# A decoder block on one core: the program's beginning in another order, with one accumulator for shift's sums

## The chip, the cores and the metric

The kernel runs on 1 core of one Trainium2 chip. The metric is device time in microseconds (us), from one execution of the program to its end; lower is better. The engines are PE (TensorE, the matmuls, with its weight loads shown as PEld), DVE (VectorE), ACT (ScalarE), POOL (GpSimd) and SP (SyncE, which here only issues DMAs). Each engine runs its own list of instructions in order and waits on semaphores for the others.

## The reference

One decoder block on 512 tokens of width 2048, float32. What matters for the beginning of the program:

```python
mod = c @ w_mod + b_mod                                   # w_mod: 2048 x 6144
shift, scale, gate = jnp.split(mod, 3, axis=-1)
u = x * (1.0 + scale[:, None, :]) + shift[:, None, :]
proj = u @ w_in                                           # w_in: 2048 x 12288
q, k, v, z_a, cb, cc, cx, z_b, g_a, g_b = jnp.split(proj, SEG_SPLITS, axis=-1)
...                                                       # attention, convolution, gated merge
out = h @ w_out
r = ALPHA * x + gate[:, None, :] * out                    # then a LayerNorm
```

## The kernel before

**Products.** Float32 products are made of rounded halves: for each weight tile ACT writes a rounded copy (`w_hi`, line 492) and DVE the remainder (`w_lo`, line 762, raw minus rounded), the same is done to the activations (`act_hi`, `act_lo`), and PE makes three matmuls of 512 columns (lines 1239 to 1241) for each product. Weights come in units of 1 MB into two slots of `raw`; a unit is two "halves", a half is 24 matmuls (6 for each of four 128-row tiles n = 0 to 3). `w_hi` and `w_lo` have four slots, so half f can be rounded once half f-4 is done. PE must have `lo_ready` for each half.

**Groups.** To begin before all of `u` is there, the program opens with eight groups g. A group takes 256 columns of `scale`: four chunks of `w_mod` (512 KB each, line 373), one pair of tiles of x (512 KB, `x_in`, line 398) and 896 KB of `w_in` (`raw`, lines 406 and 407). DVE multiplies the 16 row blocks of the chunks by `c` and adds them into two accumulators `mod_sum` in turn (lines 786 and 789, here called the sums); PE adds these over the partitions with one-column float32 matmuls (line 1288, here a reduction); DVE adds the bias (`mod`, line 808, here columns); ACT writes `act_hi` (line 537) and DVE `act_lo` (line 825) of x times (1 + scale); PE then does one half into `acc` and one gate half (18 matmuls) into `sc`. These products lack the shift, whose part is added much later by `bias_acc`.

**Then** come two halves into `misc`, the eight halves of G2 (more gate columns, f = G2 to G2+7), and the eight halves of Q0 (the first attention head, f = Q0 to Q0+7), and then the loop over heads begins (HEAD0). Beside G2 and Q0 the `shift` part of `mod` is made in the same way: 16 chunks of 1 MB (line 385), DVE's sums (512 columns wide), four reductions that PE makes ahead of the halves named in `SHIFT_BEFORE`, DVE's columns (line 816), then ACT's `add_shift` (line 564) and DVE's `shifted_lo` (line 833). Half Q0+s needs tiles 2s and 2s+1 of the shifted activations.

**Ahead of the heads.** After the fourth columns DVE does the lambda dots, the angles, `bring_down(cos)`, `bring_down(sin)` and a memset of `gate` (line 949, 2048 wide). ACT waits for that memset before it issues the DMA of `b_mod` into `gate`; then it rounds HEAD0+1 and HEAD0+2 and empties the four banks of `acc` (`drain_head`, `q_raw` first). PE's first half of HEAD0 waits for bank 0 to be emptied, by the copy to `q_raw`.

**Order.** Nothing is scheduled by a tool: each engine's order is written out by hand. SP's order is also the order of the DMAs in its one queue. `wait_raw(i, per, u)` lets unit u be loaded when the unit two before it has been subtracted; a shift chunk waits for the sums of the chunk that was in its slot.

## Time and profile before

| | us |
|---|---|
| median of 3 runs | 1517.66 (1517.55 to 1519.46) |
| the profiled execution | 1517.38 |
| its span in the profile | 1515.7 |
| PE busy | 1477.4 (97%) |
| DVE busy | 858.5 (57%) |
| ACT busy | 511.1 (34%) |
| PE's granted clock, mean | 0.995 |

A row of the timeline gives start, duration, engine, line, operation, output and inputs, the number of instructions in it, and in brackets the idle time before it with what ended it. Matmul durations overlap, since matmuls are pipelined: the time from start to start is what one costs. A granted clock of 1.00 is 2.4 GHz and 0.50 is 1.2 GHz.

### The profile page before, as it was taken

The page shows a single profiled execution, that of the slowest core. Times are in us where ns is not written, and L with a number is a line of the kernel's source. Part 1 is how long each engine was busy: PE and PEld are TensorE (multiplying, and loading weights), DVE is VectorE, ACT ScalarE, POOL GpSimd, SP SyncE. Part 2 cuts the span into 40 slices and gives each one's busy share as a digit, 9 for nine tenths or more (in the row PEclk, how much of TensorE's full clock was granted, in tenths as well). Part 3 has the DMA queues.
Part 4 walks back from the last instruction along what each step waited for, and adds up shares of the span by engine and source line. Part 5 has one row for each costly group of instructions (what it writes and reads, how often), then busy time and mean ns, then how long its engine had stood idle before and what let it go on. Part 6 is the DMA issues. An engine that isn't in the chain of part 4 may idle for free.

```text
span 1515.7 us, 18384 instructions
## 1 busy us (share of the span) xinstructions
PE 1477.4 (97%) x6624; PEld 1210.4 (80%) x6624; DVE 858.5 (57%) x1180; ACT 511.1 (34%) x721; POOL 48.7 (3%) x91
## 2 busy tenths in 40 slices
PE   4999989999999999999999999999999999999996
PEld 3888867878878788787887878888788888888885
DVE  6978657658376583765837558532532323344447
ACT  2333553354343543425444244223122221321120
POOL 0000000000000000000000000000000000000000
PEclk9999999999999999999999999999999999999998
DMA  9979525253552525525255342443223232363222
GB/s 349 392 262 383 184 70 158 79 152 90 159 159 76 154 88 159 159 84 154 81 159 159 91 153 82 161 174 106 89 84 111 83 110 84 111 249 109 86 83 111
DMA packets 211926, 219.18 MB, mean 145 GB/s; under 512 B 8369, under 2 KB 160305, under 8 KB 211121
## 3 DMA queue, kind: packets, MB, share of 16 engines
q1 hardware_dynamic: 200976, 176.75, 35.7%
q0 software_dynamic: 10096, 35.66, 7.8%
q10 hardware_dynamic: 818, 6.30, 1.0%
q8 instruction: 22, 0.36, 0.1%
q14 instruction: 14, 0.11, 0.0%
HBM read 211.33 MB, written 7.34 MB: 144 GB/s over the span
## 4 chain that ended last, share of the span: by engine, by line
PE 96%; DVE 2%; DMA 1%; ACT 0%; SPq 0%; issue 0%; DVEq 0%; ACTq 0%
PE acc L1239 30%; PE acc L1241 29%; PE acc L1240 29%; PE sc L1338 1%; PE misc L1361 1%; PE sc L1239 1%; PE sc L1241 1%; PE sc L1240 1%; DMA w_mod_in<-in_w_mod 1%; PE sc L1352 1%; PE sc L1288 0%; PE misc L1288 0%; PE misc L1344 0%; PE misc L1241 0%; PE misc L1239 0%; PE misc L1240 0%
## 5 line engine op out<-in xcount | busy, mean ns | idle before, releaser
L1239 PE MATMUL acc<-act_hi,w_hi 128*128 128x512 f32 x1472 | 578.9, 393 | 9.9 <-ACT q_raw L492 6.1
L1241 PE MATMUL acc<-act_hi,w_lo 128*128 128x512 f32 x1472 | 574.7, 390 | 0.0
L1240 PE MATMUL acc<-act_lo,w_hi 128*128 128x512 f32 x1472 | 574.6, 390 | 0.0
L492 ACT ACTIVATE w_hi<-raw 128x1024 fp32r<-128x1024 f32 (+1 forms) x256 | 268.2, 1053 | 764.7 <-PE acc L1241 618.0
L762 DVE TENSOR_TENSOR w_lo<-raw,w_hi 128x1024 fp32r<-128x1024 f32 (+1 forms) x256 | 308.7, 1214 | 379.9 <-ACT w_hi L492 379.8
L1239 PEld LDWEIGHTS acc<-act_hi,w_hi 128*128 128x128 f32 x1472 | 277.5, 189 | 71.5 <-ACT q_raw L492 6.6
L1241 PEld LDWEIGHTS acc<-act_hi,w_lo 128*128 128x128 f32 x1472 | 277.3, 188 | 58.5
L1240 PEld LDWEIGHTS acc<-act_lo,w_hi 128*128 128x128 f32 x1472 | 277.6, 189 | 57.1 <-issue 0.2
L972 DVE SCALAR_TENSOR_TENSOR bias_acc<-bias_w,mod,bias_acc 128x512 f32<-128x512 f32 x48 | 36.1, 751 | 125.7 <-DMA bias_w<-in_w_in 125.7
L1239 PE MATMUL acc<-y_hi,w_hi 128*128 128x512 f32 x256 | 99.7, 389 | 0.0
L1241 PE MATMUL acc<-y_hi,w_lo 128*128 128x512 f32 x256 | 99.6, 389 | 0.0
L1240 PE MATMUL acc<-y_lo,w_hi 128*128 128x512 f32 x256 | 99.6, 389 | 0.0
L1239 PE MATMUL acc<-w_hi,act_hi 128*128 128x512 f32 x240 | 93.4, 389 | 0.0
L1240 PE MATMUL acc<-w_lo,act_hi 128*128 128x512 f32 x240 | 93.4, 389 | 0.0
L1241 PE MATMUL acc<-w_hi,act_lo 128*128 128x512 f32 x240 | 93.4, 389 | 0.0
L789 DVE SCALAR_TENSOR_TENSOR mod_sum<-w_mod_in,c_col,mod_sum 128x256 f32<-128x256 f32 (+1 forms) x168 | 85.4, 568 | 6.2 <-DMA w_mod_in<-in_w_mod 6.1
L1240 PEld LDWEIGHTS acc<-y_lo,w_hi 128*128 128x128 f32 x256 | 48.1, 188 | 10.0
L1241 PEld LDWEIGHTS acc<-y_hi,w_lo 128*128 128x128 f32 x256 | 48.0, 188 | 10.0
L1239 PEld LDWEIGHTS acc<-y_hi,w_hi 128*128 128x128 f32 x256 | 48.1, 188 | 9.8
L623 ACT ACTIVATE prob<-sc,neg_max 128x512 f32<-128x512 f32 (+3 forms) x56 | 28.4, 519 | 73.1 <-DVE neg_max L1015 73.1
L1239 PEld LDWEIGHTS acc<-w_hi,act_hi 128*128 128x128 f32 x240 | 45.0, 188 | 9.4
L1240 PEld LDWEIGHTS acc<-w_lo,act_hi 128*128 128x128 f32 x240 | 45.0, 188 | 9.4
(174 smaller groups left out, 1081.2 us busy)
## 6 DMA issues: line engine op xcount, KB each, us to landing
raw<-in_w_in SPq DMA_DIRECT2D x256, 256.0 KB
raw<-in_w_tail SPq DMA_DIRECT2D x32, 1024.0 KB
raw<-in_w_in SPq DMA_DIRECT2D x25, 1024.0 KB
w_mod_in<-in_w_mod SPq DMA_DIRECT2D x32, 512.0 KB, 8.6
w_mod_in<-in_w_mod SPq DMA_DIRECT2D x16, 1024.0 KB, 9.3
gate_in<-in_w_mod POOLq DMA_DIRECT2D x32, 512.0 KB, 4.2
bias_w<-in_w_in POOLq DMA_DIRECT2D x48, 256.0 KB, 3.4
x_in<-in_xT SPq DMA_DIRECT2D x8, 512.0 KB, 8.5
```

Of the source, the lines that this page charges most:

```text
L492: return act.activation(dst, src, ACT.Copy)
L623: e = act.activation(prob[:, PROB_AT[t]:PROB_AT[t] + w], scores(m, t, 0, w), ACT.Exp, bias=neg_max[:, 4 * m + t:4 * m + t + 1], scale=DH * ...
L762: ins = dve.tensor_tensor(w_lo[:, f % SLOTS, :, 0:width], raw[:, (f // 2) % 2, 2 * (f % 2):2 * (f % 2) + 2, 0:width], w_hi[:, f % SLOTS, : ...
L789: dve.scalar_tensor_tensor(dst, rows[:, a, :], scale, dst, ALU.mult, ALU.add).then_inc(mod_step, 1)
L972: dve.scalar_tensor_tensor(dst, bias_w[:, :], mod[:, bass.ds(i * 2 + j // 3, 1)], dst, ALU.mult, ALU.add).then_inc(bias_free, 1)
L1239: pe.matmul(dst, a_hi, b_hi, start=first, stop=False)
L1240: pe.matmul(dst, a_hi, b_lo, start=False, stop=False)
L1241: return pe.matmul(dst, a_lo, b_hi, start=False, stop=last)
L1338: ins = pe.matmul(scores(m, t, 0, (t + 1) * P), q_f[rows, t * P:(t + 1) * P], k_f[rows, 0:(t + 1) * P], start=True, stop=True)
L1352: ins = pe.transpose(sc[:, b, c0 + (t - j) * P:c0 + (t - j + 1) * P], prob0[:, PROB_AT[t] + j * P:PROB_AT[t] + (j + 1) * P], ident)
L1361: ins = pe.matmul(misc[:, j * P:T], v_tok[:, j * P:(j + 1) * P], prob_t[:, a:a + T - j * P], start=(j == 0), stop=(j == NT - 1))
```

## The change

The order of the first 200 us is another on SP, ACT, DVE and PE; the last part of the program (heads, merges, output) is the same. SP sends the four chunks of group 0 ahead of the first pair of x and the first weights, and shift's chunks stand elsewhere between the units. ACT scales x in group 0 before it rounds the first four halves. DVE makes columns and `act_lo` of group 0 before the first subtractions; in later groups the sums of one more chunk stand between columns and `act_lo`; shift's first sums come before the columns of group 7. Shift's sums go into one accumulator, so each step waits for the one before it, and PE's reduction of shift has 4 matmuls in place of 8; it stands at other halves. x has one semaphore for each pair.

```diff
-SHIFT_BEFORE = (G2 + 2, G2 + 5, Q0 + 1, Q0 + 5)
+SHIFT_BEFORE = (G2 + 1, G2 + 4, G2 + 7, Q0 + 3)
...
-        x_landed = [sem("x_landed0"), sem("x_landed1")]
+        x_landed = [sem(f"x_landed{g}") for g in range(GROUPS)]
...
+            for c in range(MOD_CHUNKS):
+                scale_chunk(c)
+            x_pair(0)
+            pair_unit(0)
+            for g in range(1, GROUPS):
+                scale_chunk(g * MOD_CHUNKS)
+                scale_chunk(g * MOD_CHUNKS + 1)
+                x_pair(g)
+                scale_chunk(g * MOD_CHUNKS + 2)
+                pair_unit(g)
+                scale_chunk(g * MOD_CHUNKS + 3)
...
             act.sem_inc(rms_ready, BASE)
-            round_raw(0, 0, 0)
-            round_raw(1, 0, 0)
             for g in range(GROUPS):
...
-                for f in (2 * g + 2, 2 * g + 3):
+                for f in (range(SLOTS) if g == 0 else (2 * g + 2, 2 * g + 3)):
...
+            add_shift(3)
             round_at(Q0, 0, 0, 1)
-            add_shift(2)
             round_at(Q0, 0, 0, 2)
-            add_shift(3)
+            add_shift(4)
             drain_gates(1, Q0 - 1)
             round_at(Q0, 0, 0, 3)
-            round_at(Q0, 0, 0, 4)
-            add_shift(4)
-            round_at(Q0, 0, 0, 5)
             add_shift(5)
-            round_at(Q0, 0, 0, 6)
-            round_at(Q0, 0, 0, 7)
+            for s in (4, 5, 6):
+                round_at(Q0, 0, 0, s)
             add_shift(6)
             add_shift(7)
+            round_at(Q0, 0, 0, 7)
             round_at(HEAD0, 0, 0, 0)
...
-                    dst = mod_sum[:, q % 2, a % 2, 0:width]
+                    dst = mod_sum[:, q % 2, a % sums, 0:width]
...
-                        dve.wait_ge(mod_step, e - 1)
+                        dve.wait_ge(mod_step, e + 1 - sums)
...
             for n in range(MOD_CHUNKS):
                 scale_sums(0, n)
+            scale_columns(0)
+            scaled_lo(0)
             lo_half(0, 0, 0, 0)
+            scale_sums(1, 0)
             lo_half(1, 0, 0, 0)
...
+            scale_sums(1, 1)
+            scale_sums(1, 2)
+            lo_half(2, 0, 0, 0)
+            lo_half(3, 0, 0, 0)
+            scale_sums(1, 3)
+            for g in range(1, GROUPS - 1):
+                scale_sums(g + 1, 0)
                 scale_columns(g)
+                scale_sums(g + 1, 1)
                 scaled_lo(g)
...
+            lambda_dots()
             shifted_lo(6)
             shifted_lo(7)
-            dve.wait_ge(small_in, 16 * SMALL)
-            lambda_dots()
             dve.wait_ge(g_stored[0], 16)
             angles()
             bring_down(cos, 0.25)
+            lo_q(7)
+            bring_down(sin, 0.0)
             lo_half(HEAD0, 0, 0, 0)
-            bring_down(sin, 0.0)
...
-                    for a in range(2):
+                    for a in range(sums):
...
-                    reduce_sums(GROUPS + j, 4, sc[:, 0, 4 * j:4 * j + 4])
+                    reduce_sums(GROUPS + j, 4, sc[:, 0, 4 * j:4 * j + 4], 1)
```

The start of SP's list, the order of the first transfers, before:

```order
L373 DMA w_mod_in<-in_w_mod 128x4x256 x2
L398 DMA x_in<-in_xT 128x2x512
L373 DMA w_mod_in<-in_w_mod 128x4x256
L406 DMA raw<-in_w_in 128x2x512
L407 DMA raw<-in_w_in 128x2x384
L373 DMA w_mod_in<-in_w_mod 128x4x256 x3
```

and in the changed program:

```order
L373 DMA w_mod_in<-in_w_mod 128x4x256 x4
L396 DMA x_in<-in_xT 128x2x512
L406 DMA raw<-in_w_in 128x2x512
L407 DMA raw<-in_w_in 128x2x384
L373 DMA w_mod_in<-in_w_mod 128x4x256 x2
```

The fourth chunk was the last of seven transfers and is now the fourth; the seven carry the same bytes in both.

The start of DVE's list, from the sums of group 0 to the columns of group 1, before (`w_lo` of 128x1024 is an even half, 128x2x384 an odd one):

```order
L789 SCALAR_TENSOR_TENSOR mod_sum<-w_mod_in,c_col,mod_sum 128x256 x14
L762 TENSOR_TENSOR w_lo<-raw,w_hi 128x1024
L762 TENSOR_TENSOR w_lo<-raw,w_hi 128x2x384
L786 TENSOR_SCALAR mod_sum<-w_mod_in,c_col 128x256 x2
L789 SCALAR_TENSOR_TENSOR mod_sum<-w_mod_in,c_col,mod_sum 128x256 x2
L808 SCALAR_TENSOR_TENSOR mod<-misc,b_col 128x2
L825 SCALAR_TENSOR_TENSOR act_lo<-x_in,mod,act_hi 128x512 x2
L789 SCALAR_TENSOR_TENSOR mod_sum<-w_mod_in,c_col,mod_sum 128x256 x4
L762 TENSOR_TENSOR w_lo<-raw,w_hi 128x1024
```

and in the changed program, with the first reduction between its first two rows:

```order
L800 SCALAR_TENSOR_TENSOR mod_sum<-w_mod_in,c_col,mod_sum 128x256 x14
L819 SCALAR_TENSOR_TENSOR mod<-misc,b_col 128x2
L836 SCALAR_TENSOR_TENSOR act_lo<-x_in,mod,act_hi 128x512 x2
L773 TENSOR_TENSOR w_lo<-raw,w_hi 128x1024
L797 TENSOR_SCALAR mod_sum<-w_mod_in,c_col 128x256 x2
L800 SCALAR_TENSOR_TENSOR mod_sum<-w_mod_in,c_col,mod_sum 128x256 x2
L773 TENSOR_TENSOR w_lo<-raw,w_hi 128x2x384
L800 SCALAR_TENSOR_TENSOR mod_sum<-w_mod_in,c_col,mod_sum 128x256 x8
L773 TENSOR_TENSOR w_lo<-raw,w_hi 128x1024
L773 TENSOR_TENSOR w_lo<-raw,w_hi 128x2x384
L800 SCALAR_TENSOR_TENSOR mod_sum<-w_mod_in,c_col,mod_sum 128x256 x4
```

Columns and `act_lo` of group 0 moved ahead of two subtractions and the first sums of group 1; four subtractions now stand before the last sums of group 1.

DVE around the fourth columns of shift (`mod<-sc`), with the subtractions of Q0+6 and Q0+7 ahead of it, before:

```order
L833 TENSOR_TENSOR act_lo<-x_in,act_hi 128x512 x2
L762 TENSOR_TENSOR w_lo<-raw,w_hi 128x1024 x2
L816 TENSOR_TENSOR mod<-sc,b_col 128x4
L833 TENSOR_TENSOR act_lo<-x_in,act_hi 128x512 x4
L837 TENSOR_TENSOR lam_in<-lam_in 128x64
```

and in the changed program, where the two ahead of it are of Q0+5 and Q0+6:

```order
L800 SCALAR_TENSOR_TENSOR mod_sum<-w_mod_in,c_col,mod_sum 128x512 x4
L773 TENSOR_TENSOR w_lo<-raw,w_hi 128x1024 x2
L827 TENSOR_TENSOR mod<-sc,b_col 128x4
L848 TENSOR_TENSOR lam_in<-lam_in 128x64
L849 TENSOR_TENSOR lam_in<-lam_in 128x64
L851 TENSOR_REDUCE lam_dot<-lam_in 128x1
L852 TENSOR_REDUCE lam_dot<-lam_in 128x1
L844 TENSOR_TENSOR act_lo<-x_in,act_hi 128x512 x4
```

The columns moved ahead of the subtraction of Q0+7, which now stands between cos and sin; that of HEAD0, which stood there, is now behind sin.

## Rows read from the trace of the kernel before

**Rows 1.** The page, part 1: busy us, share of the span, instructions.

```profile
PE 1477.4 (97%) x6624; PEld 1210.4 (80%) x6624; DVE 858.5 (57%) x1180; ACT 511.1 (34%) x721; POOL 48.7 (3%) x91
```

**Rows 2.** Who waited for whom, PE, whole span: total us, times, longest.

```profile
PE misc L1288 <- DVE mod_sum L789: 16.9, 1, 16.9
PE acc L1239 <- ACT q_raw L492: 6.1, 1, 6.1
PE acc L1239 <- DVE act_lo L825: 3.8, 1, 3.8
```

**Rows 3.** Timeline of DVE, the first groups (L762 of 128x768 is an odd half).

```profile
11.44 1.67 DVE L789 SCALAR_TENSOR_TENSOR mod_sum<-w_mod_in,c_col,mod_sum 128x256 f32<-128x256 f32 x4 [2.57 <-DMA w_mod_in<-in_w_mod]
15.10 1.67 DVE L789 SCALAR_TENSOR_TENSOR mod_sum<-w_mod_in,c_col,mod_sum 128x256 f32<-128x256 f32 x4 [1.98 <-DMA w_mod_in<-in_w_mod]
16.69 2.08 DVE L762 TENSOR_TENSOR w_lo<-raw,w_hi 128x1024 fp32r<-128x1024 f32 x2
18.69 0.61 DVE L786 TENSOR_SCALAR mod_sum<-w_mod_in,c_col 128x256 f32<-128x256 f32 x2
...
20.01 0.15 DVE L808 SCALAR_TENSOR_TENSOR mod<-misc,b_col 128x2 f32<-128x2 f32 x1
21.06 1.41 DVE L825 SCALAR_TENSOR_TENSOR act_lo<-x_in,mod,act_hi 128x512 fp32r<-128x512 f32 x2 [0.90 <-ACT act_hi L537]
...
23.98 1.22 DVE L762 TENSOR_TENSOR w_lo<-raw,w_hi 128x1024 fp32r<-128x1024 f32 x1
25.11 1.66 DVE L789 SCALAR_TENSOR_TENSOR mod_sum<-w_mod_in,c_col,mod_sum 128x256 f32<-128x256 f32 x4
26.69 0.95 DVE L762 TENSOR_TENSOR w_lo<-raw,w_hi 128x768 fp32r<-128x768 f32 x1
27.56 1.66 DVE L789 SCALAR_TENSOR_TENSOR mod_sum<-w_mod_in,c_col,mod_sum 128x256 f32<-128x256 f32 x4
```

**Rows 4.** Timeline of ACT: rounding of the second unit, when it had landed.

```profile
22.70 1.79 ACT L492 ACTIVATE w_hi<-raw 128x1024 fp32r<-128x1024 f32 x2 [1.18 <-DMA raw<-in_w_in]
```

**Rows 5.** Timeline of PE: two reductions of scale, the first half between them.

```profile
16.91 1.83 PE L1288 MATMUL misc<-cols,mod_sum 128*128 128x1 f32 x8 [16.91 <-DVE mod_sum L789]
22.52 0.80 PE L1239 MATMUL acc<-act_hi,w_hi 128*128 128x512 f32 x1 [3.78 <-DVE act_lo L825]
...
29.83 0.95 PE L1288 MATMUL misc<-cols,mod_sum 128*128 128x1 f32 x8
30.63 0.49 PE L1239 MATMUL sc<-act_hi,w_hi 128*128 128x512 f32 x1
```

**Rows 6.** Timeline of PE: shift's fourth reduction, the end of Q0, HEAD0.

```profile
194.27 1.84 PE L1288 MATMUL sc<-cols,mod_sum 128*128 128x1 f32 x16
195.97 0.49 PE L1239 MATMUL acc<-act_hi,w_hi 128*128 128x512 f32 x1
...
212.21 0.39 PE L1241 MATMUL acc<-act_hi,w_lo 128*128 128x512 f32 x1
218.75 0.80 PE L1239 MATMUL acc<-act_hi,w_hi 128*128 128x512 f32 x1 [6.15 <-ACT q_raw L492]
...
224.03 0.46 PE L1239 MATMUL acc<-act_hi,w_hi 128*128 128x512 f32 x1
```

**Rows 7.** One window: length, busy us of PE, PEld, DVE, ACT, POOL, clock, DMA share, GB/s.

```profile
218.70:224.20 5.50, 5.46 (x13) 4.30 (x14) 2.98 (x7) 5.42 (x9) 0.00 (x0) 0.50 0.66 191
```

**Rows 8.** Timeline of DVE: shift's sums, the fourth columns, cos, the memset.

```profile
109.57 5.38 DVE L789 SCALAR_TENSOR_TENSOR mod_sum<-w_mod_in,c_col,mod_sum 128x512 f32<-128x512 f32 x8
...
196.15 0.16 DVE L816 TENSOR_TENSOR mod<-sc,b_col 128x4 f32<-128x4 f32 x1 [4.80 <-PE sc L1288]
...
206.03 1.42 DVE L862 SCALAR_TENSOR_TENSOR cos<-gate,cos 128x512 f32<-128x512 f32 x2
207.48 0.43 DVE L864 TENSOR_SCALAR cos<-cos 128x512 f32<-128x512 f32 x1
```

**Rows 9.** Timeline of ACT: bank 0 is emptied ahead of the heads.

```profile
218.12 0.58 ACT L492 ACTIVATE q_raw<-acc 128x512 f32<-128x512 f32 x1
```

More of the change, by code:

```diff
@@ L434, in _ @@
                          lams.broadcast_to([P, 4 * DH])).then_inc(small_in, 16)
+            for d in (4, 5, 6):
+                shift_chunk(d)
             gate_unit(1)
-            shift_chunk(4)
+            shift_chunk(7)
             gate_unit(2)
-            for d in (5, 6, 7):
-                shift_chunk(d)
+            shift_chunk(8)
+            shift_chunk(9)
             gate_unit(3)
-            for d in (8, 9, 10):
-                shift_chunk(d)
+            shift_chunk(10)
+            shift_chunk(11)
             first_unit(0)
-            shift_chunk(11)
             shift_chunk(12)
+            shift_chunk(13)
             first_unit(1)
-            shift_chunk(13)
             shift_chunk(14)
+            shift_chunk(15)
             first_unit(2)
-            shift_chunk(15)
             first_unit(3)
@@ L775, in _, with sum_chunk @@
             dve.wait_ge(c_in, 16)
-            def sum_chunk(q, n, rows, width):
+            def sum_chunk(q, n, rows, width, sums):
                 for a in range(MOD_STEPS):
                     e = MOD_STEPS * (MOD_CHUNKS * q + n) + a
-                    dst = mod_sum[:, q % 2, a % 2, 0:width]
+                    dst = mod_sum[:, q % 2, a % sums, 0:width]
                     scale = c_col[:, MOD_STEPS * n + a:MOD_STEPS * n + a + 1]
-                    if n == 0 and a < 2:
+                    if n == 0 and a < sums:
                         if q >= 2:
@@ L894, in lo_q @@
                 lo_half(Q0, 0, 0, s)
+            shift_sums(0)
+            scale_columns(GROUPS - 1)
+            scaled_lo(GROUPS - 1)
+            shift_sums(1)
+            lo_g(-2)
+            shift_sums(2)
+            lo_g(-1)
+            shift_sums(3)
             lo_g(0)
-            shift_sums(0)
             lo_g(1)
-            shift_sums(1)
-            shift_sums(2)
             lo_g(2)
-            shift_sums(3)
-            lo_g(3)
             shift_sums(4)
             shift_sums(5)
+            lo_g(3)
+            shift_columns(0)
+            shift_sums(6)
             lo_g(4)
-            shift_sums(6)
+            shift_sums(7)
+            shifted_lo(0)
             lo_g(5)
-            shift_columns(0)
-            shift_sums(7)
+            shifted_lo(1)
+            shift_sums(8)
             lo_g(6)
-            shift_sums(8)
-            shifted_lo(0)
+            shift_sums(9)
             lo_g(7)
-            shift_sums(9)
-            shifted_lo(1)
-            lo_q(0)
             shift_columns(1)
             shift_sums(10)
+            lo_q(0)
+            shifted_lo(2)
+            shift_sums(11)
             lo_q(1)
-            shift_sums(11)
-            shifted_lo(2)
+            shifted_lo(3)
+            shift_sums(12)
             lo_q(2)
-            shift_sums(12)
-            shifted_lo(3)
+            shift_columns(2)
+            shift_sums(13)
             lo_q(3)
-            shift_sums(13)
+            shifted_lo(4)
+            shift_sums(14)
             lo_q(4)
-            shift_columns(2)
-            shift_sums(14)
+            shifted_lo(5)
+            shift_sums(15)
             lo_q(5)
-            shifted_lo(4)
-            shift_sums(15)
-            shifted_lo(5)
             lo_q(6)
-            lo_q(7)
             shift_columns(3)
```

65 lines of the change are left out of this document (29 added, 36 removed).

## The prediction

> **What bounds the kernel now.** I read three views. The first is the page's busy shares: PE is busy 97% of the span [rows 1], so a change of order on the other engines pays only where PE stands still or does less. The second is who waits for whom, for PE over the whole span: it has three rows, 16.9 us for the first sums, 3.8 us for the first `act_lo`, 6.1 us for `q_raw` [rows 2]. So PE never waits after the first head has begun, and a microsecond that the beginning gains or loses goes into the end undiminished. The third is the timeline of each engine around these waits, to see what chain ends there.
>
> At the start the chain is: fourth chunk lands at 15.10, its sums take 1.6, then DVE does two subtractions (2.0) and the first sums of group 1 (1.3) before it comes to the columns at 20.01, although PE's reduction (16.91, 1.83 long) was done at 18.7; `act_lo` starts 1.05 later and PE's first half at 22.52 [rows 3, 5]. Ahead of the heads it is: PE has finished Q0 at 212.4, but bank 0 is emptied only at 218.12 to 218.7, and this copy ends a chain that began with the fourth columns at 196.15 and runs through DVE's cos, sin and memset; from columns to copy it is 22.0 us [rows 6, 8, 9]. After that wait PE's clock is at its lower level: granted 0.50 for 5.5 us [rows 7].
>
> **The change part by part.**
>
> (a) The start. The fourth chunk moves from the seventh place in SP's queue to the fourth. In before, the fourth transfer of 512 KB was the third chunk, and it landed at 11.44 [rows 3]. I take this for the new fourth chunk: the same bytes lie ahead of it. Its bounds are that time and the old 15.10. Sums until 11.4 + 1.6 = 13.0; reduction 0.1 + 1.8 [rows 5]; columns at 15.1. ACT then scales x, so `act_lo` runs from 16.1 (1.05 later [rows 3]); the rounding of half 0 now comes behind the scaling on ACT and ends some 2.5 after the columns (0.2, two scalings of 0.7, 0.9 for a rounding, half of the 1.79 for two in [rows 4]); subtraction of half 0 from 17.6 to 18.7 (1.13, from 23.98 to 25.11 [rows 3]). PE's first half begins near 18.9 in place of 22.52. x and the first weights are there by then, since seven transfers carry what they did and were done by 15.10.
>
> This is not the gain, for the next thing that PE needs is the reduction of group 1, and DVE now has before it: sums 1.3, odd subtraction 0.9, two chunks 3.2, subtractions 1.1 and 0.9, one chunk 1.6, all durations from start to start in [rows 3]. From 18.7 that is 27.7, reduction at 27.8. PE ends half 0 at 18.9 + 7.3 (22.52 to 29.83 [rows 5]) = 26.2 and so waits 1.6 us anew. Before, that reduction began at 29.83. Gain: 2.0 us. An earlier chunk cannot give much more: half 2 can be rounded only when the second unit has landed, at 22.70 [rows 4]; with 0.95 for the rounding, then 1.1 + 0.9 + 1.6 + 0.1 the reduction is at 27.4 at best. In later groups DVE's work is 9.5 us (the same rows added up) while PE's is 10.5, and the moved `act_lo` is ready about 4 us behind the reduction, whereas PE has 0.8 + 4.1 us of reduction and gate half first. No wait there. The waits of SP are no later than before: `wait_raw` of the third unit waits for the subtraction of half 1, now at 20.9, and the queue is the limit there.
>
> (b) Shift's reductions. 8 matmuls (16 records) took 1.70 us from start to start, 4 matmuls (8 records) 0.80 [rows 5, 6]. The changed reductions have 4. 4 x 0.9 = 3.6 us, all on PE's path.
>
> (c) The wait ahead of the heads. Three halves took from 195.97 to 212.44, so one takes 5.5 us [rows 6]. The fourth reduction moves from before Q0+5 to before Q0+3. DVE reaches the columns after the subtraction of Q0+6, which can be rounded when half Q0+2 is done, that is 5 x 5.5 + 0.8 = 28.3 us before HEAD0; with 0.2 + 1.0 for the rounding and 1.1 for the subtraction the columns are 26.0 before HEAD0, where they were 212.4 - 196.15 = 16.3 before it. The chain of 22.0 behind them has one more subtraction in it (Q0+7 between cos and sin, HEAD0 now behind sin), 1.1. The copy of bank 0 can start 2.9 us before PE needs it, and takes 0.6. The wait of 6.1 us goes, with some 2.3 us to spare. Gain 6.1. What is late next is nothing on PE: `q_rot` and `k_rot` stand to HEAD0 as they do in every head of the loop, where PE does not wait either [rows 2].
>
> (d) The clock after that wait. 12 matmuls took from 218.75 to 224.03, 5.3 us [rows 6], at a granted clock of 0.50, the level of 1.2 GHz [rows 7]; at the pace of the halves before (16.47 / 72 = 0.23 each) they take 2.75. Without the wait there is nothing to bring the clock down. Gain 2.5.
> The Trainium skill ("TensorE: Matmul & The Clock Gate", Part 1) says the same of the cause, an idle stretch throttles and activity releases, and adds that the number of slow matmuls varies from run to run. It speaks against part (a): by it the new wait of 1.6 us, if it counts as such a stretch, could slow the matmuls behind it as well.
>
> (e) One accumulator. A step on 512 columns that did not wait for its neighbour took 0.67 (5.38 for 8); two that did, in cos, took 0.72 each (206.03 to 207.48) [rows 8]. So 64 steps cost DVE 64 x 0.05 = 3.2 us over 80 us. I cost this at nothing, because the work that hides it is PE's: counting on from (a), the last sums end at about 175 where the fourth reduction is due at about 178, the third have 4 us to spare and the first two 9 and more. Bound from below nothing, since it adds work; from above, if a step took 0.8, it is 64 x 0.13 = 8 us spread over the same stretch, a good part of which falls into times where DVE waits for ACT's rounding.
>
> (f) Shift's other moves. `add_shift(4)` now stands before ACT empties the banks ahead of Q0. It can start once the third columns are made, about 4 us before Q0 is due; it takes 4 x 0.7, and the copy 0.6. That leaves 0.3 us: a loss of 0 to 0.5, I take 0. Shift's first sums stand before the columns of group 7: 2.6 us of work in a gap of 2.2, so columns 0.4 late, with 1 us of cover at the half that needs them.
>
> Sum: 2.0 + 3.6 + 6.1 + 2.5 = 14.2 us. The profiled execution of before took 1517.38, so 1503.2; its runs' median is 1517.66, 0.3 above that, so 1503.5.
>
> **The rivals.**
>
> 1. The clock falls in the new wait of 1.6 us. For: PE stands idle and has just come from the lower level. Against: there is no row of so short a wait; the two that end in slow matmuls here were 3.8 and 6.1 long [rows 2] (half 0, with the first behind it, took 7.3 us and not 5.5 [rows 5, 6]). It costs at most what (d) gives, 2.5: 1506.0.
> 2. The fourth chunk does not land earlier, because four chunks in a row move slower than three with a pair of x among them. Then the sums end at 16.7 as before, everything in (a) is 3.7 later, the reduction of group 1 at 31.5 instead of 29.83, and (a) is a loss of 1.7 in place of a gain of 2.0: 1507.2. Against it: 11.44 [rows 3] was reached with three chunks among four transfers.
> 3. The chain ahead of the heads uses up its 2.3 us, by waits of ACT behind `add_shift(6)`, `add_shift(7)` and the roundings now behind them, and PE waits again for `q_raw`, some 3 us, with part of the slow clock behind it: 1503.5 + 3 + 2 = 1508.5.
> 4. The change does not do what it says in (b): the one-column matmuls are bound by something that does not go with their number, and a reduction stays near 1.7. 1503.5 + 3.6 = 1507.1. Against: 0.80 and 1.70 for 4 and 8.
> 5. The other side, slower than before. The steps on one accumulator wait for each other's completion, and this takes far more than in cos. The place is DVE in the sums of shift; its fourth reduction has 3 us to spare, and gives time up from there: to eat 14.2 gained and lose 3 more, the 64 steps must cost 14.2 + 3 + 3 = 20.2 us more, 0.32 each, a step of 0.99 us. The point from which the kernel is slower at all is (14.2 + 3) / 64 = 0.27, a step of 0.94. At 1.1 it would be 64 x 0.43 - 3 = 24.5 us on top of 1503.5, 1528. Against it stand the 0.72 of [rows 8].
>
> **How the numbers follow.** Forecast, within 1.5 us of 1503.5: 0.66. Rival 1: 0.09. Rival 2: 0.08. Rival 3: 0.06. Rival 4: 0.03. Rival 5: 0.03. Small new waits or two of the rivals together, which end between 1508 and 1516: 0.05. The range reaches from 1501.7 (everything at its best bound: 27.4 for the reduction, fewer slow matmuls at the start, a faster run) to 1507.8, which takes in rivals 1, 2 and 4; some 0.14 is left out. A difference of 0.2%, 3 us, is about what a measurement of this kernel can tell from no change. All rivals but the fifth stay more than that below before, so faster 0.92; within 0.2%, from the mixed cases, 0.04; slower 0.04.
>
> **What would show it.** The timeline of the changed kernel: first sums of the fourth chunk near 11.4 and not 15.1; PE's second reduction near 27.8 with a wait for DVE's sums of 1 to 2 us before it; four reductions of shift with 8 records and 0.8 us; HEAD0's first matmul at once behind Q0, near 207, with no row for `q_raw` in PE's waits, and granted clock 1.00 there; dependent steps of 0.72 in shift's sums. The prediction is wrong if PE's waits show a new row above 2 us, at Q0's start, at a shift reduction or at HEAD0, or if DVE's steps are longer than 0.8.

## The result, and the profile after

The changed kernel takes 1508.78 us, median of four runs (1507.05 to 1510.98), against 1517.63 for the kernel before, timed in the same rounds. The ratio is 0.9941, with a 95% interval of 0.9929 to 0.9954: faster by 8.9 us. The forecast was 1503.5 with a range of 1501.7 to 1507.8. So the sign was right, and the median lies 1.0 us above the range: 14.2 us were reckoned, and 8.9 came.

The profiled execution took 1508.81 with a span of 1507.2, 8.5 us less than the span before. Its busy shares and PE's waits (engine, line, waited for: total us, times, longest):

```profile
PE 1474.7 (98%) x6592; PEld 1207.6 (80%) x6592; DVE 863.1 (57%) x1180; ACT 510.7 (34%) x721; POOL 48.4 (3%) x91
```

```profile
PE misc L1307 <- DVE mod_sum L800: 14.2, 2, 12.6
PE acc L1258 <- issue: 3.9, 1, 3.9
PE acc L1258 <- ACT g_out L505: 2.9, 1, 2.9
```

Beside [rows 2] this says most of it. The row for `q_raw` is gone. The first wait has become two, 12.6 before the first reduction and 1.5 before the second. And there is a row of 2.9 us that the prediction did not have: PE waits at the start of Q0 until ACT has emptied a bank into `g_out`. Line 1307 is the reduction of before's line 1288, 1258 to 1260 the matmuls of 1239 to 1241, 800 the sums of 789, 505 the copies and roundings of 492.

**The start.** PE's timeline, which answers to [rows 5]:

```profile
12.64 1.84 PE L1307 MATMUL misc<-cols,mod_sum 128*128 128x1 f32 x8 [12.64 <-DVE mod_sum L800]
18.42 0.76 PE L1258 MATMUL acc<-act_hi,w_hi 128*128 128x512 f32 x1 [3.95 <-issue]
...
27.32 1.05 PE L1307 MATMUL misc<-cols,mod_sum 128*128 128x1 f32 x8 [1.53 <-DVE mod_sum L800]
29.17 0.63 PE L1258 MATMUL sc<-act_hi,w_hi 128*128 128x512 f32 x1
...
39.46 0.95 PE L1307 MATMUL misc<-cols,mod_sum 128*128 128x1 f32 x8
```

The second reduction stands at 27.32 where before had 29.83 [rows 5], 2.5 us earlier. From 29.17 the matmuls behind it start 0.43 apart and not 0.23. Two windows (length, busy us of PE, PEld, DVE, ACT and POOL, granted clock, DMA share, GB/s), the first over these slow ones, the second over those behind them:

```profile
28.80:31.90 3.10, 3.10 (x9) 2.45 (x8) 2.81 (x6) 1.91 (x3) 0.00 (x0) 0.50 1.08 390
31.90:39.40 7.50, 7.50 (x34) 6.19 (x33) 6.66 (x14) 1.22 (x2) 0.00 (x0) 0.98 1.07 395
```

PE is busy throughout, at 0.50 of its clock in the first, the level of 1.2 GHz, and at nearly all of it in the second. The third reduction stands at 39.46 and stood at 40.30 in before (the row is further down, with the place where time is lost again), so of the 2.5 us 0.84 is left.

**Q0's start.** The timelines of ACT and DVE, then of PE:

```profile
119.05 2.01 ACT L505 ACTIVATE w_hi<-raw 128x1024 fp32r<-128x1024 f32 x2 [9.95 <-DMA raw<-in_w_in]
...
163.16 0.82 ACT L575 ACTIVATE act_hi<-x_in,mod 128x512 fp32r<-128x512 f32 x1 [4.65 <-DVE mod L827]
...
166.00 2.02 ACT L505 ACTIVATE g_out<-acc 128x512 f32<-128x512 f32 x4
```

```profile
120.14 1.23 DVE L773 TENSOR_TENSOR w_lo<-raw,w_hi 128x1024 fp32r<-128x1024 f32 x1 [10.66 <-ACT w_hi L505]
121.29 0.48 DVE L797 TENSOR_SCALAR mod_sum<-w_mod_in,c_col 128x512 f32<-128x512 f32 x1
121.80 5.54 DVE L800 SCALAR_TENSOR_TENSOR mod_sum<-w_mod_in,c_col,mod_sum 128x512 f32<-128x512 f32 x7
...
162.97 0.16 DVE L827 TENSOR_TENSOR mod<-sc,b_col 128x4 f32<-128x4 f32 x1
```

```profile
163.41 0.39 PE L1260 MATMUL acc<-act_hi,w_lo 128*128 128x512 f32 x1
166.71 0.47 PE L1258 MATMUL acc<-act_hi,w_hi 128*128 128x512 f32 x1 [2.91 <-ACT g_out L505]
```

Read from the bottom: PE wants bank 0 empty at 163.8. ACT begins to empty it only at 166.00, since `add_shift(4)` stands ahead of that copy and runs from 163.16. `add_shift(4)` waits for the third columns, made at 162.97. DVE is late with these since it stood 10.66 us, until 120.14, for weights that had not landed. The 7 steps of the sums, in the third row of DVE, start (5.54 - 0.76) / 6 = 0.80 us apart; in the longer rows it is 0.79.

**Ahead of the heads.** Columns, the copy of bank 0, the clock:

```profile
185.59 0.15 DVE L827 TENSOR_TENSOR mod<-sc,b_col 128x4 f32<-128x4 f32 x1
```

```profile
208.04 0.58 ACT L505 ACTIVATE q_raw<-acc 128x512 f32<-128x512 f32 x1
```

```profile
215.00:222.00 7.00, 7.00 (x33) 5.76 (x31) 4.75 (x7) 6.09 (x9) 0.00 (x0) 1.00 0.00 0
```

The fourth columns come at 185.59 and came at 196.15 [rows 8], the copy at 208.04 and was at 218.12 [rows 9]. PE does not wait, and its clock is whole where [rows 7] has 0.50. From 166.71, eight halves of 5.45 us and one reduction of 0.8 put the start of HEAD0 near 211.1, so the copy starts some 3 us before it; 2.9 were reckoned.

**Where time is lost again.** Some 760 us later, behind 24 records of one-column matmuls that reduce `bias_acc`, the changed kernel's PE timeline and a window, and then PE in the kernel before at the third reduction of scale and at this place:

```profile
970.99 2.73 PE L1408 MATMUL misc<-cols,bias_acc 128*128 128x1 f32 x24
...
974.85 0.63 PE L1259 MATMUL acc<-y_lo,w_hi 128*128 128x512 f32 x1
```

```profile
974.40:977.80 3.40, 3.40 (x10) 2.65 (x9) 0.00 (x0) 0.00 (x0) 2.06 (x3) 0.51 0.68 229
```

```profile
40.30 0.94 PE L1288 MATMUL misc<-cols,mod_sum 128*128 128x1 f32 x8
...
981.10 2.73 PE L1389 MATMUL misc<-cols,bias_acc 128*128 128x1 f32 x24
...
984.73 0.39 PE L1240 MATMUL acc<-y_lo,w_hi 128*128 128x512 f32 x1
```

No line of the diff is near it. The clock fell for 3.4 us, with PE busy before, in and behind the reduction; in before it did not. It costs about 1.6 us, and the gain shows it: the reduction itself comes 10.1 us earlier (981.10 to 970.99), the end of the span 8.5.

The difference of the two profiled executions, in us:

| place | reckoned | found |
|---|---|---|
| second reduction of scale earlier | +2.0 | +2.5 |
| clock falls behind it | 0 (rival 1) | -1.7 |
| four reductions of shift, 8 records for 16 | +3.6 | +3.6 |
| wait at Q0's start | 0 | -2.9 |
| wait ahead of the heads | +6.1 | +6.1 |
| slow clock behind that wait | +2.5 | +2.5 |
| clock falls behind the `bias_acc` reduction | not seen | -1.6 |
| sum | 14.2 | 8.5 |

### The profile page after: what moved, and what is told of

It reads as the page before. It is cut to its first block, busy times and chain, and to the rows that moved or that the text cites. A ratio compares the mean times of both kernels' runs of the same rounds, so it can differ in the third digit from the quotient of the medians.

```text
span 1507.2 us, 18320 instructions
## 1 busy us (share of the span) xinstructions
PE 1474.7 (98%) x6592; PEld 1207.6 (80%) x6592; DVE 863.1 (57%) x1180; ACT 510.7 (34%) x721; POOL 48.4 (3%) x91
## 4 chain that ended last, share of the span: by engine, by line
PE 92%; DVE 4%; DMA 1%; issue 1%; ACT 1%; SPq 0%; DVEq 0%; ACTq 0%
PE acc L1258 29%; PE acc L1260 29%; PE acc L1259 29%; DVE mod_sum L800 3%; PE sc L1357 1%; PE misc L1380 1%; DMA raw<-in_w_in 1%; DVE w_lo L773 1%; PE sc L1371 1%; PE sc L1258 1%; PE sc L1260 0%; PE sc L1259 0%; PE misc L1307 0%; DMA w_mod_in<-in_w_mod 0%; DVE act_lo L844 0%
## 5 line engine op out<-in xcount | busy, mean ns | idle before, releaser
L800 DVE SCALAR_TENSOR_TENSOR mod_sum<-w_mod_in,c_col,mod_sum 128x256 f32<-128x256 f32 (+1 forms) x172 | 92.1, 577 | 2.3 <-DMA w_mod_in<-in_w_mod 0.5
L1258 PEld LDWEIGHTS acc<-y_hi,w_hi 128*128 128x128 f32 x256 | 48.4, 189 | 10.1
L1260 PEld LDWEIGHTS acc<-w_hi,act_lo 128*128 128x128 f32 x240 | 45.1, 188 | 9.3
```

Of the source, the lines that this page charges most:

```text
L800: dve.scalar_tensor_tensor(dst, rows[:, a, :], scale, dst, ALU.mult, ALU.add).then_inc(mod_step, 1)
L1258: pe.matmul(dst, a_hi, b_hi, start=first, stop=False)
L1260: return pe.matmul(dst, a_lo, b_hi, start=False, stop=last)
```

## The experiments

The theory after reading both traces: the late weights and the place of `add_shift(4)` make the wait at Q0's start; the waits and the one-column matmuls make the clock fall. The main rival for the wait is that the longer steps on one accumulator do it; the rival for the clock is that it falls by chance, whatever stands there. Each ratio is against the kernel before in the same rounds (1517.58, 1517.52 and 1517.47 in the three batches). The changed kernel was not timed again beside them; its 1508.78 stands against a before of 1517.63, so differences between an experiment and the changed kernel rest on medians of before that agree within 0.2 us. Unless it says "before", the edit is made to the changed kernel.

**1. The second gate unit ahead of two chunks of shift (e1_unit_ahead).** In SP's program:

```diff
-            for d in (4, 5, 6):
-                shift_chunk(d)
+            shift_chunk(4)
             gate_unit(1)
-            shift_chunk(7)
+            for d in (5, 6, 7):
+                shift_chunk(d)
```

> The changed kernel with one edit: on SP the second gate unit (the weights of G2+2 and G2+3) is sent ahead of shift's chunks 5 and 6, and not behind them. In the changed kernel it was issued at 104.21 and landed at about 119.0, 14.8 us later; ACT, in order, waited 9.95 us for it, DVE 10.7 us, and PE later 2.9 us at the start of Q0. Theory (place in the queue): the unit lands 5 us or more earlier, DVE's wait there falls from 10.7 to some 4 to 6 us, the third columns come 3 us or more earlier and PE's wait at Q0 is under 0.5 us: about 1505.9 us. Rival (the dependent steps of DVE, 0.79 us each, set the third columns): the unit lands earlier, but PE's wait at Q0 stays above 2 us: about 1508.5 us. Either way a clock fall behind the twelve one-column matmuls near 970 us may or may not come, 1.6 us.

1504.34 us (1503.63 to 1505.2), ratio 0.9912, 0.9895 to 0.9928: 4.4 us under the changed kernel, all four runs below its fastest. First the DMA issues on SP's queue in the changed kernel (the time is that of the issue, not of the transfer), and below them those of this one:

```profile
98.92 4.53 SPq L385 DMA_DIRECT2D w_mod_in<-in_w_mod  x2
104.21 0.40 SPq L391 DMA_DIRECT2D raw<-in_w_in  x1
107.24 0.37 SPq L385 DMA_DIRECT2D w_mod_in<-in_w_mod  x1
```

```profile
104.49 0.41 SPq L391 DMA_DIRECT2D raw<-in_w_in  x1
104.95 2.94 SPq L385 DMA_DIRECT2D w_mod_in<-in_w_mod  x3
```

The unit is issued at the same time in both, since SP waits for its buffer. What differs is what lies in front of it: two chunks of 1 MB issued from 98.92 on. By the chain of waits of the changed kernel the unit took 14.76 us to land:

```profile
104.21 14.76 DMA raw<-in_w_in
```

The window over this time in the changed kernel:

```profile
104.20:119.00 14.80, 14.80 (x67) 12.27 (x66) 5.18 (x6) 3.83 (x7) 1.65 (x2) 1.00 1.04 412
```

The engines were full, and moved 14.8 us x 412 GB/s = 6.1 MB. The unit is 1.0 of them, the two chunks in front at most 2.1, POOL's stores from `gate` and `g_out` (issued at 106.13 and 109.41) 1.8; what is left must be of the loads that SP issued behind it, at 107.24 and 109.51. That POOL's stores take from the same engines as SP's loads is what the Trainium skill says ("DMA: Bandwidth & Descriptors", Issuing engines are not separate DMA queues); the totals here agree, but no run took the stores away.

With the unit ahead, ACT's and DVE's next roundings in this kernel:

```profile
112.37 1.06 ACT L505 ACTIVATE w_hi<-raw 128x1024 fp32r<-128x1024 f32 x1 [2.97 <-PE misc L1260]
```

```profile
113.47 1.23 DVE L773 TENSOR_TENSOR w_lo<-raw,w_hi 128x1024 fp32r<-128x1024 f32 x1 [3.71 <-ACT w_hi L505]
```

```profile
128.36 1.06 ACT L505 ACTIVATE w_hi<-raw 128x1024 fp32r<-128x1024 f32 x1 [9.05 <-DMA raw<-in_w_in]
```

```profile
PE acc L1258 <- ACT g_out L505: 0.6, 1, 0.6
```

The unit has landed when ACT comes to it at 112.37 (ACT waits for PE, as elsewhere), DVE loses 3.7 us in place of 10.7, and of the 2.9 us at Q0's start 0.6 is left. Of the 2.3 us gone, 2.0 come from the third columns, at 160.94 and not 162.97; the other 0.3 is PE's own, which is that much later from the third reduction of scale on (39.77 and not 39.46). So the late unit made about two thirds of this wait, 2.0 of 2.9. The columns did not come the 3 us earlier that were expected, since the lateness moved on: the next unit is the late one now, and ACT waits 9.05 us for it, as the second ACT row shows. The other 2 us or so by which this kernel is faster are not the wait's: in its profile the clock did not fall behind the `bias_acc` reduction.

**2. Two accumulators again (e2_two_sums).**

```diff
-                sum_chunk(GROUPS + j, n, shift_in(d), COLS, 1)
+                sum_chunk(GROUPS + j, n, shift_in(d), COLS, 2)
...
-                    reduce_sums(GROUPS + j, 4, sc[:, 0, 4 * j:4 * j + 4], 1)
+                    reduce_sums(GROUPS + j, 4, sc[:, 0, 4 * j:4 * j + 4], 2)
```

> The changed kernel with shift's sums on two accumulators again, everything else as it is. The steps do not wait for their neighbours (0.66 in place of 0.79 us, some 0.5 us less for a chunk) and a reduction has 8 matmuls again (1.7 us in place of 0.8). Theory (queue): the unit lands at 119 as before, but the nine chunks of sums between there and the third columns cost 4.5 us less, so PE's wait at Q0 falls from 2.9 to under 0.5, and the four reductions cost 3.6 us more: about 1508.8 - 2.9 + 3.6 = 1509.5 us. Rival (the length of the steps does not matter there, since DVE waits for ACT): the wait of 2.9 us stays: about 1512.4 us.

1508.93 (1507.6 to 1510.44), ratio 0.9941, 0.9924 to 0.9957: the same as the changed kernel. One accumulator brought nothing there that the runs can tell. Neither theory had it right: the wait is gone, as the first says, but not by the 4.5 us that it put down to DVE. DVE and ACT in this kernel:

```profile
121.46 1.23 DVE L773 TENSOR_TENSOR w_lo<-raw,w_hi 128x1024 fp32r<-128x1024 f32 x1 [11.28 <-ACT w_hi L505]
...
162.74 0.16 DVE L827 TENSOR_TENSOR mod<-sc,b_col 128x4 f32<-128x4 f32 x1
```

```profile
165.77 1.55 ACT L505 ACTIVATE g_out<-acc 128x512 f32<-128x512 f32 x3
167.80 0.60 ACT L505 ACTIVATE g_out<-acc 128x512 f32<-128x512 f32 x1 [0.48 <-PE acc L1260]
```

The unit is as late, the columns hardly earlier (162.74), and yet PE does not wait at Q0. It comes there later itself: by 1.28 since this run's third reduction is at 40.74 and not 39.46 (its first chunk landed later, a first reduction at 13.89), and by 2.7 for three reductions of 16 records ahead of Q0. That is 4.0 against a wait of 2.9. DVE's shorter steps are a smaller part: the columns came 0.23 earlier, or 1.5 if the late start is taken out. So in the changed kernel most of the gain of three reductions of shift was turned into the wait at Q0: PE was let run ahead of a chain that did not get shorter.

**3. `add_shift(4)` behind the emptying of the banks (e3_add4_behind).**

```diff
-            add_shift(4)
             drain_gates(1, Q0 - 1)
+            add_shift(4)
```

> The changed kernel with one edit on ACT: the fifth add_shift (p = 4) stands behind the emptying of the gate banks ahead of Q0, not before it. Theory: PE's wait at Q0 is this order's price, the banks wait for the third columns only through add_shift; with the edit they are emptied as soon as they are full, the wait is under 0.3 us and no wait appears at Q0+4, whose act_lo has four halves more: about 1506.0 us. Rival: the wait is only moved, to a half of Q0 or to the fourth reduction, and the time stays within 0.5 us of 1508.8.

1505.84 (1502.92 to 1506.61), ratio 0.9925, 0.9908 to 0.9941: 2.9 us under the changed kernel, as expected, all four runs below its fastest. ACT now, in place of 166.00:

```profile
162.72 0.60 ACT L505 ACTIVATE g_out<-acc 128x512 f32<-128x512 f32 x1 [0.76 <-PE acc L1260]
163.21 0.81 ACT L575 ACTIVATE act_hi<-x_in,mod 128x512 fp32r<-128x512 f32 x1
```

Banks are emptied as PE finishes them, and PE has no row for `g_out`. The unit is as late here (ACT waits 10.25 for it): the wait needs the late unit and the order on ACT together, and either remedy takes all or most of it. In this execution the clock did not fall before PE's last matmul (1489.44), and it took 1502.92; the other three runs took 1505.19 to 1506.61. Its PE at the start:

```profile
27.44 1.05 PE L1307 MATMUL misc<-cols,mod_sum 128*128 128x1 f32 x8 [0.98 <-DVE mod_sum L800]
...
29.15 0.40 PE L1258 MATMUL sc<-act_hi,w_hi 128*128 128x512 f32 x1
29.38 0.39 PE L1259 MATMUL sc<-act_lo,w_hi 128*128 128x512 f32 x1
```

**4. The kernel before with one accumulator for shift and nothing else (e4_one_sum_alone).** The edit of experiment 2 turned round, in before.

> The kernel of before with one edit: shift's sums on one accumulator, reductions of 4 matmuls. Theory: the reductions take 0.8 in place of 1.7 us each, and all of it is on the path, since the chain to the wait ahead of the heads begins behind the fourth reduction: the wait of 6.1 us stays and the time falls by 3.6 us, to about 1514.0. DVE's steps take 0.79 and not 0.66 us. Rival: DVE's longer steps make a reduction late: new waits at shift's reductions, gain below 2 us.

1514.03 (1512.8 to 1515.66, ten runs), ratio 0.9977, 0.9967 to 0.9986: 3.5 us faster. Steps and reductions, DVE and PE:

```profile
109.45 6.33 DVE L789 SCALAR_TENSOR_TENSOR mod_sum<-w_mod_in,c_col,mod_sum 128x512 f32<-128x512 f32 x8
```

```profile
191.48 0.95 PE L1288 MATMUL sc<-cols,mod_sum 128*128 128x1 f32 x8
...
215.06 0.80 PE L1239 MATMUL acc<-act_hi,w_hi 128*128 128x512 f32 x1 [6.14 <-ACT q_raw L492]
```

Eight steps take 6.33 where [rows 8] has 5.38: 0.79 each and not 0.67. Where nothing waits for DVE, this costs nothing, and the 3.6 of term (b) come whole. The wait for `q_raw` is as long as before. The profiled execution took 1514.39, 3.0 less than before's: 3.6 from the reductions, 0.8 since the first 12 matmuls behind the wait took 4.4 and not 5.3, and 1.6 lost because here the clock fell behind the `bias_acc` reduction.

**5. The kernel before with the new start and nothing else (e5_start_alone).** SP sends all four chunks of group 0 first, then x and the first unit; DVE takes the columns ahead of the subtractions; ACT scales x ahead of the rounding.

A piece of the edit:

```diff
+            for c in range(MOD_CHUNKS):
+                scale_chunk(c)
+            x_pair(0)
+            pair_unit(0)
```

> The kernel of before with the order of the first eight groups of the changed kernel alone (SP's transfers, ACT's and DVE's lists up to the columns of group 7; shift as before, on two accumulators). Theory: the third reduction of scale (R2) begins at 38.2 to 39.5 in place of 40.30, by 2.1 us where the clock stays up in the new wait at the second reduction and by 0.8 where it falls; all that follows, the wait of 6.1 us ahead of the heads included, is moved by that: 1515.5 to 1517 us, median some 1.3 under before. Rival: the sums of one more chunk between columns and act_lo make a later group late, or the wait ahead of the heads takes the gain: 1517.5 or more.

1516.06 (1515.16 to 1517.98, ten runs), ratio 0.9993, 0.9983 to 1.0002. By the medians this is 1.5 us faster, but the interval includes no change at all. In its profile the second reduction stood at 28.17 behind a wait of 0.69, the clock did not fall, and the third came at 38.70, 1.6 earlier than before. The start is worth less than the forecast's 2.0 and is the least certain part of the change. In the eight profiles that have the new start without the swap of experiment 6, the third reduction comes from 2.1 us earlier (e3) to 0.4 later (e2) than before's 40.30, 1.0 earlier on average.

**6. Group 1's sums ahead of a subtraction (e6_start_swap).**

```diff
-            lo_half(3, 0, 0, 0)
             scale_sums(1, 3)
+            lo_half(3, 0, 0, 0)
```

> The changed kernel with one edit at the start: DVE makes the last sums of group 1 ahead of the subtraction of half 3, not behind it, so the second reduction of scale can begin 0.9 us earlier. In the changed kernel PE ended half 0 at 25.6, the reduction began at 27.32 and the clock was at 0.50 from 28.8 to 31.9. Theory: reduction at 26.4, wait 0.7 in place of 1.5; the third reduction at 37.5 to 37.8 with the clock up, 1.7 us earlier than 39.46, and at 38.6 if it falls all the same: median 1 to 1.8 us under 1508.8. Rival: half 3 comes late, or the third reduction is set by the landing of the weights for group 2 (31.2), not by the second reduction: gain under 0.5 us.

1508.03 (1506.8 to 1509.83), ratio 0.9944, 0.9928 to 0.9959: by time no different from the changed kernel, and short of the 1 to 1.8 us expected. The swap does what it says: from first to second reduction it is 13.82 us and not 14.68. But the first reduction was at 13.37 here and not 12.64, so the second came at 27.19 and not at 26.4. In its profile the wait before the second reduction is 0.43, the clock stays whole and the third is at 37.97, the earliest of all; but it has the wait at Q0 (2.5) and the fall at the `bias_acc` reduction.

**7 to 10. The remedies together.** The 12 one-column matmuls of the `bias_acc` reduction (24 records) were split in three lots of four, with the matmuls of a gate half between, and DVE's copy of the result one half later:

```diff
-                if s == 8:
+                if s < 11:
...
-                    for n in range(SPILLED):
+                    for n in range(4 * (s - 8), 4 * (s - 8) + 4):
...
-                    ins.then_inc(bias_reduced, 1)
+                    if s == 10:
+                        ins.then_inc(bias_reduced, 1)
```

e8 has the edits of 1 and 3, e7 these and the split, e9 these, the split and the swap of 6, e10 the split alone.

> The changed kernel with the edits of the two runs before it together (gate unit ahead of shift's chunks 5 and 6; add_shift 4 behind the emptying of the gate banks), and the twelve one-column matmuls of bias_acc, which stood in a row behind half A0+8, as four each behind A0+8, A0+9 and A0+10. In the changed kernel's profile 24 records of 2.6 us in all were followed by a granted clock of 0.50 for some 3 us, 1.6 us lost; in the profile of before they were not. Theory: no profile shows that fall any more, and the median is 0.5 to 1.6 us under the same kernel without the split (next run). Rival: the fall has to do with something else at that place: the median is the same within 0.3.

> The changed kernel with the two edits together, gate unit ahead of shift's chunks 5 and 6, and add_shift 4 behind the emptying of the gate banks; the one-column matmuls as they were. Both edits aim at the same wait of 2.9 us at Q0, of which the first left 0.6 and the second 0. Theory: together they give what the second gives, 1505.8 less the tenths by which the first helps, 1504 to 1505.5, no wait at Q0. Rival: their gains add up (3.5 + 3 us): 1502.5.

> The changed kernel with four edits together: gate unit ahead of shift's chunks 5 and 6, add_shift 4 behind the emptying of the gate banks, the twelve one-column matmuls of bias_acc in three lots of four, and at the start the last sums of group 1 ahead of the subtraction of half 3. Theory: no wait of PE after the third reduction of scale, the second reduction with under 0.5 us of wait, no fall of the clock behind it nor behind the one-column matmuls; third reduction of scale near 38.1; 1502.5 us, runs within 1.5 us of each other. Rival (the start's swap gives nothing beside the others): the same as without it, 1503.4.

> The changed kernel with one edit, the twelve one-column matmuls of bias_acc in three lots of four. Theory: the fall of the clock at that place, 1.6 us when it comes, comes no more, so the median falls from 1508.8 to about 1507.5 and the profile shows a granted clock of 1.00 from 960 to 990 us. Rival: the fall is not bound to the row of 24 records; the profile shows it in some other place of this stretch, or the median does not move.

| kernel | median | lowest to highest | ratio, 95% interval |
|---|---|---|---|
| e7_unit_add4_split | 1503.36 | 1502.28 to 1503.75 | 0.9907, 0.9892 to 0.9922 |
| e8_unit_add4 | 1506.18 | 1504.11 to 1506.77 | 0.9926, 0.9912 to 0.9939 |
| e9_all_four | 1502.46 | 1501.68 to 1502.88 | 0.9900, 0.9885 to 0.9915 |
| e10_split_alone | 1508.53 | 1506.8 to 1511.09 | 0.9946, 0.9933 to 0.9960 |

e9 is the fastest kernel of the study, 15 us under the kernel before and 6.3 under the changed one. PE's waits in it are those of the start alone, and the window that the split concerns is at full clock; below them that window in e8, where the matmuls stand in a row:

```profile
PE misc L1307 <- DVE mod_sum L800: 13.9, 2, 13.5
PE acc L1258 <- issue: 3.9, 1, 3.9
```

```profile
960.00:990.00 30.00, 30.00 (x145) 25.16 (x144) 11.49 (x13) 8.76 (x11) 2.78 (x4) 1.00 0.56 196
```

```profile
960.00:990.00 30.00, 30.00 (x139) 25.10 (x138) 10.64 (x13) 7.27 (x9) 2.78 (x4) 0.94 0.63 219
```

Against what was expected: e9 met its 1502.5. It is 0.9 us under e7, and the runs of the two overlap, so what the swap is worth there stays open. e8 missed its 1504 to 1505.5 by 0.7, and lies 0.3 above e3. e7 is 2.8 us under e8, which differs from it by the split alone; that is more than the 0.5 to 1.6 expected, but e8's profile also has a fall of the clock at the start that e7's has not. e10 missed its 1507.5: the split alone moved the median by 0.25 us, which settles nothing. Its profiled execution shows the full clock there, and took 1506.80 with the other two losses in place; its other four runs took 1508.10 to 1511.09, at a mean clock of 0.995 or 0.996 against 0.997. Where they lost more no profile shows.

**The clock, over all profiles.** One profiled execution of each kernel that has the new start, by the wait before the second reduction of scale. The last column counts the matmuls of half 0 that start 0.43 us apart and not 0.23; they come ahead of the wait.

| kernel | wait | second, third reduction | between | clock behind the wait | slow in half 0 |
|---|---|---|---|---|---|
| e9 | 0.36 | 27.32, 38.12 | 10.8 | whole | 9 |
| e6 | 0.43 | 27.19, 37.97 | 10.8 | whole | 9 |
| e5 | 0.69 | 28.17, 38.70 | 10.5 | whole | 12 |
| e3 | 0.98 | 27.44, 38.20 | 10.8 | whole | 11 |
| e7 | 1.01 | 28.48, 39.05 | 10.6 | whole | 11 |
| changed | 1.53 | 27.32, 39.46 | 12.1 | falls | 8 |
| e8 | 1.65 | 27.17, 39.30 | 12.1 | falls | 7 |
| e2 | 1.75 | 28.57, 40.74 | 12.2 | falls | 7 |
| e10 | 1.82 | 26.96, 39.10 | 12.1 | falls | 6 |
| e1 | 1.86 | 27.60, 39.77 | 12.2 | falls | 6 |

A fall costs 1.3 to 1.7 us here. The last column sorts the ten as well as the wait does: 6 to 8 slow matmuls with a fall, 9 to 12 without. The two go together, since in the eight kernels without the swap the second reduction stands 14.68 or 14.69 us behind the first, so that the earlier the clock rises in half 0, the longer PE then waits. Whether the fall comes from the length of the wait or from the time at which the clock rose, these runs can't tell. (For the slow matmuls of half 0 the clock of the windows reads 1.00, in the changed kernel too, and only their spacing shows the level.)

```profile
18.40:21.90 3.50, 3.48 (x8) 2.80 (x9) 3.50 (x9) 0.09 (x1) 0.00 (x0) 1.00 1.07 397
```

Behind 24 one-column records in a row it fell in five executions (the changed kernel, e2, e4, e6, e8) and not in four (before, e1, e3, e5); with the matmuls split it fell in none of three. If the split did nothing and five falls fell on twelve profiles by chance, none of them would hit these three in 0.16 of the cases.

**Do the pieces add up?** From the changed kernel's 1508.81, with each execution's own third reduction, its own wait at Q0, 1.6 us less where the clock did not fall at the `bias_acc` reduction, and for e2 3.6 more:

| kernel | start | wait at Q0 | `bias_acc` | reckoned | profiled execution |
|---|---|---|---|---|---|
| e1 | +0.3 | -2.3 | -1.6 | 1505.2 | 1505.20 |
| e2 | +1.3 | -2.9 | 0 | 1510.8 | 1510.44 |
| e3 | -1.3 | -2.9 | -1.6 | 1503.0 | 1502.92 |
| e6 | -1.5 | -0.4 | 0 | 1506.9 | 1506.97 |
| e7 | -0.4 | -2.9 | -1.6 | 1503.9 | 1503.75 |
| e8 | -0.2 | -2.9 | 0 | 1505.7 | 1505.44 |
| e9 | -1.3 | -2.9 | -1.6 | 1503.0 | 1502.88 |
| e10 | -0.4 | -0.2 | -1.6 | 1506.6 | 1506.80 |

All eight come within 0.4 us. Three places explain what these profiled executions differ by. They are one run of each kernel, and the runs of one kernel lie up to 4.3 us apart (e10).

## Why the prediction was right and wrong

The step that failed is term (f): `add_shift(4)` can start "about 4 us before Q0 is due", so "a loss of 0 to 0.5, I take 0". In the run it could start 0.8 us before, and PE waited 2.9. That is also what the prediction named as a sign of being wrong, a new row above 2 us at Q0's start. Two further losses make up the rest: the clock fell in the new wait of (a), put at nothing in the sum and kept as rival 1, for 1.7 us, and it fell behind the `bias_acc` reduction, which the prediction does not have, for 1.6. Together they are 6.2 of the 14.2 us reckoned, and the start gave 0.5 more than reckoned ahead of its fall.

- **What bounds the kernel**: right. PE is busy 98% of the span, and what the beginning gains goes into the end, less what is lost on the way. The step "PE never waits after the first head has begun, and a microsecond goes into the end undiminished" left out that a busy PE can still be slowed: 1.6 us at the `bias_acc` reduction. That reduction is in the trace of before too, at a clock of 1.00, so that trace alone did not tell it.
- **(a), 2.0**: the mechanism was right, row by row. The fourth chunk lands with the third's old time (first reduction at 12.64, 13.1 reckoned), PE's first half begins at 18.42 (18.9 reckoned), the second reduction at 27.32 (27.8) behind a wait of 1.53 (1.6). The term was mis-sized by what follows the wait. It is 2.5 - 1.7 = 0.8 in this execution and 1.6 in e5's, where the clock stays; the 2.0 is reached in one profile of eight, e3's. **Rival 1** is what happened: I gave it 0.09 and a price of at most 2.5. It cost 1.3 to 1.7, and came in five executions of ten, in each with a wait above 1.5 us. The argument against it was that no row showed so short a wait; that was absence of evidence. The Trainium skill ("TensorE: Matmul & The Clock Gate", Part 1) has the number of slow matmuls vary from run to run, and the ten rows above bear it out: 6 to 12 in half 0, and behind the wait some or none.
- **(b), 3.6**: right. Four reductions of 8 records at 0.79 to 0.80; e4 alone shows 3.5. **Rival 4** fell.
- **(c) and (d), 6.1 and 2.5**: right in size and cause. The fourth columns are 10.6 us earlier, PE does not wait, the clock stays. HEAD0 came near 211 and not near 207, by what was lost ahead of it. **Rival 3** fell.
- **(e), nothing**: wrong. "A step takes 0.72" was 0.79, which lay inside the bound that I had named ("if a step took 0.8"). The slack was the larger error: "the third have 4 us to spare" was counted on from (a) with the second gate unit in time. It landed at 119.0, and DVE stood for 10.7 us. What (e) lacks is SP's queue: I walked PE, DVE and ACT forward but not that queue past the start, where two chunks of shift now lie ahead of that unit and POOL's stores beside it.
- **(f), "0 to 0.5, I take 0"**: wrong, 2.9. The working itself gave little cover: 0.3 us as written, and 4 - 2.8 - 0.6 = 0.6 by its own numbers, from the same 4 us of slack that (e) counted. That slack was about 0.8 in the run (columns at 162.97, PE at Q0 at 163.8), so nearly all of the 2.8 us of `add_shift(4)` and the copy became wait. Experiments 1 and 3 take the wait away from either end. Even with the unit ahead (experiment 1) 0.6 us of wait is left, so the slack is short of what the two operations take.
- **Rivals 2 and 5** fell. The fourth chunk landed early. A step of 0.79 is far from the 0.94 from which the kernel would be slower.
- **The range** held each mishap alone, and the sum of three ran past it. I gave 0.05 to "small new waits or two of the rivals together".

## What to carry to other kernels

When a change moves transfers forward, walk the DMA queue forward too, as far as the next buffer that an engine rounds from, and count every byte in front of it, the other queues' stores included. A saving on the engine that sets the time is kept only if the chain it waits on next has slack: with slack one accumulator gave 3.5 us (experiment 4), without it nothing that the runs can tell (experiment 2). And put a copy that frees a bank ahead of work that waits for another engine's result, where both are in one engine's order.

## What the runs showed of the hardware that I had not expected

- PE's clock fell behind a wait of 1.53 to 1.86 us that ended in 8 one-column records, and not behind one of 0.36 to 1.01; yet in the profiles it did not fall behind the wait at Q0 that ended in full matmuls (2.9 us in the changed kernel, 2.5 in e6, 2.7 in e10). The length of the first wait goes with the time at which the clock rose in half 0, so the table does not show that the length decides. The windows of the wait at Q0 and of what came behind it, in the changed kernel:

```profile
163.80:166.70 2.90, 0.00 (x1) 0.02 (x1) 2.26 (x3) 2.90 (x6) 0.00 (x0) 1.00 0.23 70
166.70:173.00 6.30, 6.29 (x28) 5.20 (x29) 3.94 (x6) 5.62 (x9) 0.75 (x1) 1.00 0.49 171
```

- It fell behind 2.6 us of one-column matmuls with no idle time at all, in five of nine executions. Both places have one-column matmuls in common, and the fall was absent in all three executions with the row of 24 split. That they are its cause is not shown, and three profiles are few: no run put full matmuls in their place or lengthened the wait alone, and of the unsplit ones four of nine did not fall either.
- Steps on DVE that each wait for their neighbour start 0.79 us apart, against 0.67 for those that wait for the step before their neighbour (128x512, [rows 8] and experiment 4), 0.72 in cos. The Trainium skill ("VectorE: DVE Perf Modes", The DRAIN you can't avoid) has it that a semaphore after each operation costs nothing extra, measured on copies. In both orders here every step signals and waits, and what differs is which step it waits for; waiting for the neighbour costs 0.12 us a step, so the sentence does not carry over to steps that add to what the neighbour has just written.
- The first chunks of `w_mod` land up to 1.6 us apart from run to run (first reduction from 12.28 to 13.89 in ten profiles), which no part of the change explains; the latest two stand on either side of the clock's table (e2 fell, e7 at 13.80 did not).
